# The on-chip buffers of a two-layer decoder kernel allocated in another order, so that the large ones begin at multiples of 2,048 bytes

## The reference

```
for i in range(2):
    x = x + 0.5 * swiglu_ffn(rmsnorm(x), ffn1_w_in[i], ffn1_w_out[i])    # 1024 -> 2 x 2816 -> 1024
    h = rmsnorm(x)
    mk, mv = split(rmsnorm(mem) @ mem_w_kv[i])
    z = h @ w_in                                # i = 0: HGRN2, i = 1: chunked gMLP; last 1024 columns: queries
    o_mix = hgrn2_mixer(...)  if i == 0 else  chunked_spatial_gating(...)
    x = x + concat(o_mix, memory_attention(zx, mk, mv)) @ w_out
    x = x + 0.5 * swiglu_ffn(rmsnorm(x), ffn2_w_in[i], ffn2_w_out[i])
return rmsnorm(x)
```

## Time and profile before

| what | value |
|---|---|
| median of three runs | 2417.21 us (2416.2 to 2417.99) |
| the profiled execution, its own time | 2418.09 us |
| its span, first to last instruction | 2416.4 us |
| PE busy | 2398.8 us (99% of the span), 10,944 matmuls |
| DVE, ACT, POOL busy | 1198.7, 742.8, 263.1 us |
| DMA | 234.32 MB, mean 97 GB/s |

### The profile page before, as it was taken

How to read it: one execution, slowest core, us unless ns; L and a number is a source line. 1 busy time by engine, 2 the same in 40 slices (tenths; PEclk the granted TensorE clock), 3 DMA queues, 4 the chain that set the end, 5 groups by cost and what they waited for, 6 DMA issues and landing times.

```text
span 2416.4 us, 29488 instructions
## 1 busy us (share of the span) xinstructions
PE 2398.8 (99%) x10944; PEld 1943.4 (80%) x10944; DVE 1198.7 (50%) x1411; ACT 742.8 (31%) x1005; POOL 263.1 (11%) x235
## 2 busy tenths in 40 slices
PE   9999999999999999999999999999999999999998
PEld 9988888877888778888878888877788887888887
DVE  6654443446888554444345444334337644444422
ACT  4432222234444322222222222223323222222322
POOL 3400001101333310000110000210001111000000
PEclk9999999999999999999999999999999999999999
DMA  7633333332222333333323333333232233333222
GB/s 234 206 93 95 95 89 94 95 105 62 70 78 70 100 93 96 95 90 92 96 88 95 95 95 91 92 95 96 70 96 85 81 96 97 95 95 95 89 94 88
DMA packets 400692, 234.32 MB, mean 97 GB/s; under 512 B 7693, under 2 KB 386673, under 8 KB 400625
## 3 DMA queue, kind: packets, MB, share of 16 engines
q1 hardware_dynamic: 397328, 223.37, 31.4%
q0 software_dynamic: 3280, 10.02, 1.2%
q10 hardware_dynamic: 16, 0.00, 0.0%
HBM read 227.07 MB, written 6.29 MB: 97 GB/s over the span
## 4 chain that ended last, share of the span: by engine, by line
PE 95%; DVE 2%; ACT 1%; issue 1%; DMA 1%; POOL 0%; DVEq 0%; ACTq 0%; SPq 0%; POOLq 0%
PE acc L1012 27%; PE acc L1014 27%; PE acc L1013 26%; PE acc L766 1%; PE acc L768 1%; PE acc L767 1%; PE mix L398 1%; PE mix L385 1%; PE acc L250 1%; PE acc L249 1%; PE acc L251 1%; PE mix L251 1%; PE mix L250 1%; PE mix L249 1%; ACT w_hi L1444 1%
## 5 line engine op out<-in xcount | busy, mean ns | idle before, releaser
L1174 DVE TENSOR_TENSOR w_lo<-raw,w_hi 128x1024 fp32r<-128x1024 f32 (+1 forms) x422 | 546.3, 1297 | 676.2 <-ACT w_hi L1444 665.6
L1012 PE MATMUL acc<-h_hi,w_hi 128*128 128x512 f32 x1920 | 771.9, 402 | 6.1 <-DVE h_lo L1236 3.8
L1014 PE MATMUL acc<-h_hi,w_lo 128*128 128x512 f32 x1920 | 759.8, 396 | 0.0
L1013 PE MATMUL acc<-h_lo,w_hi 128*128 128x512 f32 x1920 | 755.9, 394 | 0.0
L1444 ACT ACTIVATE w_hi<-raw 128x1024 fp32r<-128x1024 f32 (+1 forms) x422 | 436.5, 1038 | 368.5 <-DMA raw<-in_ffn_w_out_dram 232.2
L1012 PEld LDWEIGHTS acc<-h_hi,w_hi 128*128 128x128 f32 x1920 | 361.1, 188 | 93.1 <-DVE h_lo L1236 5.2
L1014 PEld LDWEIGHTS acc<-h_hi,w_lo 128*128 128x128 f32 x1920 | 360.7, 188 | 89.8
L1013 PEld LDWEIGHTS acc<-h_lo,w_hi 128*128 128x128 f32 x1920 | 361.0, 188 | 88.9 <-issue 3.1
L1012 PE MATMUL acc<-act_hi,w_hi 128*128 128x512 f32 (+1 forms) x976 | 373.8, 383 | 2.1 <-DVE act_lo L1185 1.0
L1014 PE MATMUL acc<-act_hi,w_lo 128*128 128x512 f32 (+1 forms) x976 | 372.6, 382 | 0.0
L1013 PE MATMUL acc<-act_lo,w_hi 128*128 128x512 f32 (+1 forms) x976 | 369.5, 379 | 0.0
(11 more groups left out here) (214 smaller groups left out, 1785.5 us busy)
## 6 DMA issues: line engine op xcount, KB each, us to landing
raw<-in_ffn_w_in_dram SPq DMA_DIRECT2D x176, 512.0 KB, 3.8
raw<-in_ffn_w_out_dram SPq DMA_DIRECT2D x70, 512.0 KB, 4.1
raw<-in_hgrn_w_in_dram SPq DMA_DIRECT2D x40, 512.0 KB, 3.8
raw<-in_gmlp_w_in_dram SPq DMA_DIRECT2D x40, 512.0 KB, 3.7
raw<-in_mem_w_kv_dram SPq DMA_DIRECT2D x32, 512.0 KB, 4.2
raw<-in_gmlp_w_out_dram SPq DMA_DIRECT2D x24, 512.0 KB, 4.1
raw<-in_ffn_w_out_dram SPq DMA_DIRECT2D x24, 384.0 KB, 3.5
raw<-in_hgrn_w_out_dram SPq DMA_DIRECT2D x16, 512.0 KB, 4.1
```

The costliest lines, as they stand in the source:

```text
L1012: pe.matmul(bank, w_hi[:, j, i, :], hi, start=(start and i == 0), stop=False)
L1013: pe.matmul(bank, w_hi[:, j, i, :], lo, start=False, stop=False)
L1014: m = pe.matmul(bank, w_lo[:, j, i, :], hi, start=False, stop=(stop and i == last))
L1174: dve.tensor_tensor(w_lo[:, j, 0:nkb], raw[:, j, 0:nkb], f32(w_hi[:, j, 0:nkb]), ALU.subtract).then_inc(w_lo_ready, 1)
```

## The change

Six calls are moved, and nothing else. The instructions of every engine, their order and their waits are the same in both programs. Only addresses differ.

```diff
+        ident = sb("ident", [P, P])
+        ones = sb("ones", [P, P])
+        q_row = sb("q_row", [P, P])
+        small = sb("small", [P, 96])
         x = sb("x", [P, DB, T])
 
         with nc.sbuf_tensor("raw", [P, LANES, KU, P], F32) as raw:
             pass
         w_lo = sb("w_lo", [P, LANES, KU, P], F32R)
         w_hi = sb("w_hi", [P, LANES, KU, P], F32R)
-        ident = sb("ident", [P, P])
-        ones = sb("ones", [P, P])
-        vecs = sb("vecs", [P, NROWS])
         rstd = sb("rstd", [P, T])
         sq = sb("sq", [P, 2, T])
         tmp = sb("tmp", [P, 6, T])
         pair = sb("pair", [P, 2, T])
         bs_all = sb("bs_all", [P, GROUPS, P])
-        q_row = sb("q_row", [P, P])
-        small = sb("small", [P, 96])
...
         work = sb("work", [P, 48, T])
+        vecs = sb("vecs", [P, NROWS])
```

## The result

The changed kernel takes 2362.44 us, the median of five runs (2361.65 to 2363.06), beside 2417.21 for the kernel before in the same comparison. The ratio is 0.9772, with a 95% interval of 0.9758 to 0.9786. It is 55 us faster, and the prediction of 2417.0 us, "same", was wrong by all of it. The edit moves five calls of `sb` (ident, ones, q_row, small and vecs), not six.

The account below looks back on a forecast made before the run. PE was taken as the bound, 9,216 matmuls by their spacing. Matmuls 0, DVE, ACT and POOL 0 and weight loads -0.2 us gave 2417.9, or 2417.0 us on the median's scale; own range 2415 to 2419, 8 in 10 within 2410 to 2424.

Parts of the forecast that it names:

- same: Whole kernel: a time within 0.2%, 4.8 us, of no change, given a chance of 0.74.
- What bounds the kernel: Whole span: PE is busy 99%, its waits total 10.3 us, so time is 9,216 matmuls multiplied by their spacing.
- Matmuls with new operand addresses, value 0: All PE matmuls: spacing stays at 233.3 ns, value 0, with bounds of +7.5 and -184 us.
- The four observations: Trace evidence on addresses: stationary slices, moving operands, swapped roles, and one line at two speeds with the same layout.
- The first two: Weight slices and kv moving blocks: those straddling a multiple of 2,048 take the same 0.70 and 0.36 us as others.
- The third: L766, where weights move and h is stationary: 234.2 ns, 0.9 ns more than with the roles the other way round.
- The fourth observation: L1056, 256 columns, one layout: 117.3 and 120.0 ns, a 2% difference without any difference in addresses.
- DVE, ACT and POOL: Work beside the matmuls: equal remainders cost at most 5 ns per instruction, all covered, value 0.
- Weight loads: Loads landing at multiples of 512 bytes: bounds -2 us and 0, value taken -0.2 us.
- Rival A: All matmuls: the 20 ns come from operands not beginning on some large boundary and go, 2233 us; chance 0.04.
- Rival C: Stream of L1012 to L1014: accesses of equal remainder are served one behind the other, 7.5 us slower, 2424.5; chance 0.13.
- 0.13 for faster: Whole kernel: chance of a faster result, from A at 0.04 and B, transfers and swapped roles gaining, at 0.09.

Follow-up runs that it names:

- e1: Streams of fp32r matmuls alone, the computation left out, at various moving and stationary start bytes: spacing 226.7 ns at (0, 0), 233.3 ns at (480, 128).
- e4: The changed kernel with 64 bytes ahead of x, so all large buffers begin at remainder 64 by 2,048: 2361.33 us, ratio 0.9764.
- e7: Streams of matmuls alone, mapping moving starts in 16-byte steps with the stationary operand at 0, plus other widths: 226.7 to 234.6 ns at 512 columns.
- e9: The changed kernel with the normed memory 192 bytes further inside the activation buffers, for the 256-column matmuls of kv: 2360.64 us, ratio 0.9762.
- e5: The kernel before with a pad of 160 bytes ahead of h, so h and activations begin at 640, weights at 128: 2364.33 us, ratio 0.9773.
- e8: The changed kernel with 160 bytes ahead of h, so h and activations begin at 160, weights at 0: 2424.14 us, ratio 1.0024.
- e6: The changed kernel with 32 bytes ahead of x, so all large buffers begin at remainder 32: 2361.21 us, ratio 0.9759.
- e10: Streams of matmuls alone, trying the lower clock, 4-byte steps, alternating slices, narrower blocks and bf16: 426 and 427 ns at the lower clock, bf16 215.8 ns.

## Why the prediction was wrong, point by point

**What bounds the kernel: right.** PE bound it end to end, and the whole change is in the spacing. The sum as count by spacing holds: 9,216 x 6.7 ns = 61 us, and 56 us of the span went.

**Matmuls with new operand addresses, value 0: the step that failed.** The prediction bounded the cost by +7.5 and -184 us and took "the row that the operands are nearest to, the 233.3 ns of the same line with other remainders". The measured value is -6.7 ns per matmul. The four observations were read rightly and proved less than was drawn from them. The first two tested straddling, and straddling has in fact no cost (e1, e4). The third swapped the roles, which turns a difference of 96 (480 - 128 = 352) into one of 160: 233.7 and 234.4 ns in the map of e7. Both layouts of the trace lay on the plateau of 233 to 234.6 ns, so near each other that they looked like one constant. In the kernel before, moving and stationary operand of every fp32r matmul had a difference of 96 or 160 by 256, and no row could show the valley at 240 to 0. The fourth observation (two speeds of L1056 in one layout, with 256 columns) is right, and e9 has the same, but it was used to discard the 0.9 ns of the third, and these were real: the streams of 512 columns have them too. Where a trace holds only two values of a cause, it is no evidence that the cause has no effect.

**DVE, ACT and POOL: right.** 692 and 689 ns after, 693 and 688 before. e5 has the whole gain with the temporaries at 1632.

**Weight loads: right that nothing is won.** The first load takes 6.21 us, before 6.15. By the Trainium skill ("DMA: Bandwidth & Descriptors", section "How a descriptor splits into AXI transactions"), had its rule for reads held for these writes, it would have fallen by about 1.2 us, the prediction's estimate from that page, and it didn't.

**Rival A** had the sign and the place (the 20 ns, or a part of them, go) and the wrong cause and size. It took the loss for one of straddling or of a boundary and gave 2233 us. Of the 20 ns above 213.3 a third goes, and at least 13.3 ns stay at every difference that was tried with 512 columns. The spacing that the Trainium skill gives ("TensorE: Matmul & The Clock Gate", section "Wait — 56ns, not 53.3ns?"), 215.7 ns, is what bf16 has here (215.8), not fp32r. **Rival C** was wrong for the change: with 512 columns equal remainders are the best case and not the worst. A slower kernel of its size, 6 us, exists (e8), by the difference of 160.

**What was given back.** Of 61 us, about 5 don't arrive. The waits of PE grow by 2.5 us. And the granted clock falls twice to its lower level after such waits, where it fell once before. The windows of the kernel after, with PEclk behind the five engines:

```profile
479.00:487.00 8.00, 7.72 (x25) 5.56 (x26) 5.56 (x5) 4.52 (x5) 2.01 (x3) 0.79 0.81 281
1230.00:1238.00 8.00, 5.91 (x17) 3.92 (x16) 5.32 (x5) 4.77 (x5) 2.79 (x3) 0.79 0.23 68
```

Before the first of these spells PE waits 2.2 us for h_lo, and before the second 2.1 us. Not every such wait is followed by a fall: the 2.2 us for w_lo ahead of the first FFN were in the kernel before and aren't here. The other kernels that have the gain show two such spells (e6) or three (e4, e5) in their profiles. The timeline of PE behind the first shows starts 0.43 us apart at difference 0, as they were at difference 96 in the earlier trace rows:

```profile
482.35 0.63 PE L1013 MATMUL acc<-h_lo,w_hi 128*128 128x512 f32 x1
482.78 0.63 PE L1014 MATMUL acc<-h_hi,w_lo 128*128 128x512 f32 x1
```

One spell more at the lower level costs about 8 matmuls x 200 ns = 1.6 us. That leaves about 1 us, the size of what the 384 matmuls of kv's v quads lose where 117.3 ns became 120.0 (384 x 2.7 ns = 1.0 us, an estimate, since waits of kv may have absorbed a part of it).

**The chances.** 0.13 for faster was too little for a change whose only open quantity multiplies 9,216 matmuls and had 20 unexplained ns in each. A gain of 2 ns would have been enough to leave "same" behind.

## What to carry to other kernels

With fp32r matmuls of 512 columns, make the moving and the stationary operand begin at multiples of 32 bytes and at the same remainder by 256. For other widths measure, since their maps differ (e7, e9, e10). A pad of a few bytes between two buffers does it (e5), and one in the wrong place undoes it (e8). Check the spacing of a long stream against columns divided by the clock: what stands above it without a wait is a quantity to be measured in a small kernel of streams, not one to be reasoned away. A layout's effect on one operand can't be read from a trace in which all operands keep their distances.

## What the runs showed of the hardware that I had not expected

- With the stationary operand at a multiple of 32, the spacing of fp32r matmuls with 512 columns depends on the difference of the two operands' start addresses, with a period of 256 bytes: 226.7 ns at 0 and 240, up to 234.6 ns elsewhere on multiples of 16, and up to 239.9 ns off them. The streams with the stationary operand at 4 and 16 don't follow this map (e1).
- With 256 columns the best value seen is 113.3 ns. Of four streams at difference 192 one has it and three have 117.8 ns (e10), and in e9 both values stand at the same start addresses by 256.
- The dependence isn't there in bf16 (215.8 ns at all differences), nor at the lower clock (426.7 ns at difference 96 and at 0).
- fp32r matmuls of 128 and of 192 columns both take 111.7 ns from start to start.
- Even at the best difference fp32r has 544 cycles for 512 columns. What the 32 cycles are stays open, and so does the mechanism: it was neither proportional to the width of the slice (e7) nor bound to the own or the next slice alone (e10).
